# Earlier first loads in a diffusion-step kernel: w_ada and x weights of the heads in the shared stage, four expert blocks beside w_out, first picks between the first products

## The chip, the cores and the metric

The kernel runs on one core of a Trainium2 chip. Times are device microseconds of a whole execution of the program. The three runs of the kernel before took 2437.72, 2439.86 and 2441.40 us. The profile comes from a further execution, and its stage times are counted in microseconds from the start of its span.

## The reference

One layer of a network that mixes two kinds of state-space heads and ends in a mixture of experts is applied to a prompt of 128 tokens and to a sample of 256 tokens. All is float32, the model width D is 2048, and the prompt and the sample have modulation vectors of their own. In outline, for one token set x:

```
mod  = silu(cond) @ w_ada + b_ada                      # six vectors of 2048: shift, scale, gate, twice
h    = rms_norm(x) * (1 + scale_m) + shift_m
proj = h @ w_in                                        # widths: z 1024, x 1024, B and C 512, dt 32, then RWKV
y    = [ ssd_heads(z, conv(x), conv(B, C), dt),  rwkv7_heads(...) ]     # 16 + 16 heads, forward and backward
x    = x + gate_m * (y @ w_out)
h    = rms_norm(x) * (1 + scale_f) + shift_f
aff  = softmax(h @ router_w)                           # 16 experts
gate, idx = top_k(aff.T, 2 * n_tok / 16)               # each expert picks 16 prompt and 32 sample tokens
hid  = silu(h[idx] @ w_gate[e]) * (h[idx] @ w_up[e])   # 2048 -> 1024, for e = 0 .. 15
x    = x + gate_f * scatter_add((hid @ w_down[e]) * gate)
out  = rms_norm(x) * g                                 # besides: the final states of all heads
```

The weights of the experts are 16 x 24 blocks of 1024 KB (8 of gate, 8 of up and 8 of down for each expert), each read once.

## The kernel before, in words

The 384 tokens (T) are handled at once; activations lie with the channels on the 128 partitions. A large tile, `arena`, holds three tensors of 16 x 384 columns: `xT` (the residual), `mixed` (the outputs of all heads) and `hT` (the normed input). Each stage is a block with one instruction list for each engine, written out by hand: SP issues loads from its queue in the order of the code, POOL issues the w_ada loads of the heads from a software queue, and semaphores carry the waits. Between stages all engines meet at a barrier. A load that was issued before a barrier may land behind it, where its user waits for its semaphore.

The stages in order:

- **setup** (to about 106 us): reads the vectors, transposes x, and computes the first two modulation vectors from 32 blocks of w_ada.
- **ssd_shared** (106 to 222 us): projects dt, B, C and the low-rank inputs of RWKV. TensorE's `project(n, ...)` (L413 to L417) multiplies `w_shared` block n by `hT`; six blocks go through a ring of five (L377, L399 to L402), each with its semaphore `loaded[n]`. Then SP loads the first x and z weights of the heads into the two slots of `w_xz` (L403, L404). TensorE projects these at L449 to L453 (semaphores `x_proj`, `z_proj`). POOL only clears two tiles (L408, L409). `mixed` isn't in use before the heads write it.
- **ssd_heads** (222 to 515 us): eight turns, one for each pair of heads. In a turn TensorE does the x and z projections of the next pair (`feed`, 32 steps of K), the attention-like products of the pair, and, spread between them, eight `strips` of the remaining four modulation vectors: strip n multiplies `cond` by `wa[:, n % 4]`, one of four slots of w_ada blocks. POOL opens with twelve semaphore increments (`ahead`, the last one is `adah_col`, for which the first strip waits), then issues the loads: four at once, and each later one when a slot was used. SP opens with small loads (decay rows to memory and back: `seg`, `eac`), then loads the x weights of the second pair (`if c == 0`), then the second z weights, and so on in turn.
- **rwkv** (to about 1292 us): the second kind of heads; the first part of the w_out product is done in its last turns.
- **project_out** (1292 to 1430 us): the rest of the w_out product, 16 chunks of output channels through a ring of four (L1576), with residual, transposition back to tokens, and the router's products. SP issues the last load when chunk 11 is done, and then waits only for `gfin`.
- **experts** (1431 us to the end): `route()` ranks the tokens; `pick(g)` gathers the tokens of four experts by one-hot products, 16 steps of k, each evicted by VectorE (prompt part) and ScalarE (sample part) into `picked`; then for each expert `up` (8 steps kk, each with a gate and an up block), `turn`, `down` (8 blocks). The blocks run through a ring of 12 slots: 6 in `arena` (over `xT` and `mixed`) and 6 in `w_exp`. SP issues the load of block g when block g - 12 was used (`exp_used`, L1731 to L1737). `up(0)` waits for all 16 evictions of `pick(0)`:

```
                if e == 0 or e in PICK_AT:
                    pe.wait_ge(S("picked_c"), KC * (PICK_AT.get(e, 0) + 1))
                    pe.wait_ge(S("picked_s"), KC * (PICK_AT.get(e, 0) + 1))
```

Of the kernel before, what the change touches and what calls it, by code (L numbers as in the profile page):

```python
# [21 lines left out]
P = 128  # L22
D = 2048
KC = D // P
# [92 lines left out]
def program(nc, I, O, table, stop="all"):  # L117
# [17 lines left out]
    with ctx:  # L135
        ps = [ctx.enter_context(nc.psum_tensor(f"bank{n}", [P, 512], F32)) for n in range(8)]
        cst = sb(ctx, "cst", [P, CONST["row"][0]])
        par = sb(ctx, "par", [P, 352])
        modT = sb(ctx, "modT", [P, 96, 2])
        gain = sb(ctx, "gain", [P, 2, KC, 2])  # L140
        cond = sb(ctx, "cond", [P, KC, 32])
        arena = sb(ctx, "arena", [P, 3 * KC * T])
        xT, mixed, hT = (arena[:, n * KC * T:(n + 1) * KC * T].rearrange("p (k t) -> p k t", k=KC) for n in range(3))
        xtok = arena[:, 2 * KC * T:].rearrange("p (t d) -> p t d", t=TILES)

        def C(name, p0=0, p1=P):
            a, b = CONST[name]
            return cst[p0:p1, a:b]

        env = dict(nc=nc, I=I, O=O, table=table, S=S, sb=sb, ps=ps, cst=cst, par=par, modT=modT, gain=gain, xT=xT, C=C)  # L150
        with ExitStack() as proj:
            lora = sb(proj, "lora", [P, 3, T])
            w_narrow = sb(proj, "w_narrow", [P, KC, P])
            setup(**env, cond=cond, hT=hT, w_narrow=w_narrow)
            if stop == "ada":
                return
            ssd(**env, cond=cond, hT=hT, mixed=mixed, lora=lora, w_narrow=w_narrow)
            if stop == "ssd":
                return
            reuse_semaphores()  # L160
            rwkv(**env, hT=hT, mixed=mixed, lora=lora)
        reuse_semaphores()
        if stop == "rwkv":
            return
        with ExitStack() as ffn:
            acc = sb(ffn, "x_sum", [P, KC * T])
            late = dict(gates=sb(ffn, "gates", [P, D // 2]), gfin=sb(ffn, "gfin", [P, D]), shifts=sb(ffn, "shifts", [P, 48]),
                        acc=acc, sums=acc[:, 0:T], logits=acc[0:48, T:2 * T], xtok=xtok)
# [180 lines left out]


def ssd(nc, I, O, table, S, sb, ps, cst, par, modT, gain, xT, C, cond, hT, mixed, lora, w_narrow):

    w_in = I["w_in"].rearrange("l (k p) n -> p (l k) n", p=P)
    with ExitStack() as st:
# [11 lines left out]
        w_xz = sb(st, "w_xz", [P, 2, KC, P])  # L366
        ssd_shared(nc, I, S, sb, ps, par, modT, gain, xT, C, hT, lora, w_narrow, w_xz, w_in, B, Cm, Btok, BC, cum, ea, r7, tokq, cin, acc, sig)
        ssd_heads(nc, I, O, S, sb, ps, par, modT, C, cond, hT, mixed, w_xz, w_in, Cm, Btok, BC, cum, ea, r7, tokq, cin, acc, sig)


def ssd_shared(nc, I, S, sb, ps, par, modT, gain, xT, C, hT, lora, w_narrow, w_xz, w_in, B, Cm, Btok, BC, cum, ea, r7, tokq, cin, acc, sig):

# [3 lines left out]
    with ExitStack() as st:  # L376
        RING = 5  # L377
        w = sb(st, "w_shared", [P, RING, KC, P])
        dt = sb(st, "dt", [HEADS, 2, T])
# [14 lines left out]
        def _(sp):  # L394
# [16 lines left out]
        @block.tensor  # L411
# [163 lines left out]

def ssd_heads(nc, I, O, S, sb, ps, par, modT, C, cond, hT, mixed, w, w_in, Cm, Btok, BC, cum, ea, r7, tokq, cin, acc, sig):

    HG = KC // 4
    with ExitStack() as st:
# [14 lines left out]
        y = sb(st, "y", [P, T])  # L594
        AR, SLOTS_A = 4, 8
# [3 lines left out]
        w_ada = I["w_ada"].rearrange("l (k p) n -> p (l k) n", p=P)  # L599
        block = st.enter_context(nc.Block())  # L600
# [3 lines left out]
        def _(pool):  # L604
            ahead(pool, S, "z_proj", "hT_in", "sT_out", "s1_ready", "y_done", "xtok_in", "x_conv", "fin_out", "y_in", "adah_col")

            def load(c, n):
                src = w_ada[:, 2 * n:2 * n + 2, bass.ds(c * 1024 + 2 * D, 1024)]
                nc.gpsimd.dma_start(wa[:, n % AR], src).then_inc(ada_loaded[n % AR], 16)
# [19 lines left out]
        def _(sp):  # L629
# [917 lines left out]

def project_out(nc, I, O, table, S, sb, ps, cst, par, modT, gain, xT, C, mixed, gates, gfin, acc, sums, logits, shifts, xtok):

# [6 lines left out]
    with ExitStack() as st:  # L1556
# [15 lines left out]
        def _(sp):  # L1572
            for n in range(KC):
# [106 lines left out]

def experts(nc, I, O, table, S, sb, ps, cst, par, modT, gain, xT, C, arena, gates, gfin, acc, sums, logits, shifts, xtok):

# [9 lines left out]
    PICK_AT = {PACK * g: g for g in range(1, PACKS)}  # L1692
    wide = [I[n].rearrange("l e (q c p) n -> p (l e q) c n", p=P, c=2) for n in ("exp_w_gate", "exp_w_up")]
    tall = I["exp_w_down"].rearrange("l e (q p) n -> p (l e q) n", p=P)
    with ExitStack() as st:
        more = sb(st, "w_exp", [P, RING - HOME, 2048])
        w = [arena[:, n * 2048:(n + 1) * 2048] for n in range(HOME)] + [more[:, n] for n in range(RING - HOME)]
        picked = sb(st, "picked", [P, KC, PACK * SLOTS + PAD])
# [28 lines left out]
        def _(sp):  # L1727
            for e in range(N_EXP):
                for n in range(NS):
                    g = e * NS + n  # L1730
                    if g >= RING:  # L1731
                        sp.wait_ge(S("exp_used"), g - RING + 1)
                    if n < UPS:
                        dst, src = w[g % RING].rearrange("p (c n) -> p c n", c=2), wide[n % 2][:, e * 8 + n // 2]
                    else:
                        dst, src = w[g % RING], tall[:, e * 8 + n - UPS]
                    sp.dma_start(dst, src).then_inc(loaded[g % RING], 16)  # L1737
            for i in range(TILES * 4):
# [7 lines left out]
        def _(pe):  # L1746
            def arrived(e, n):
                g = e * NS + n
                pe.wait_ge(loaded[g % RING], (g // RING + 1) * 16)
                return w[g % RING]  # L1750
# [16 lines left out]

            def pick(g):

                pe.wait_ge(S("onehot"), min(g, 1) + 1)  # L1770
                if g:
                    pe.wait_ge(S("gu_out"), 2 * PACK * g)
                    pe.wait_ge(S("G"), PACK * g)
                for k in range(KC):
# [4 lines left out]
                    pe.matmul(ps[k % 2][:, 0:PACK * CAPC], xtok0(k), ohc[:, PACK * g:PACK * (g + 1)].rearrange("p e c -> p (e c)"), start=True, stop=True).then_inc(S("pick_c"), 1)  # L1779
                    for t in range(2):  # L1780
# [67 lines left out]
            route()  # L1848
            pick(0)
            for e in range(N_EXP):  # L1850
# [78 lines left out]
        def _(dve):  # L1929
# [43 lines left out]
            def pick(g):  # L1973
                for k in range(KC):
                    dve.wait_ge(S("pick_c"), KC * g + k + 1)
                    V.tensor_scalar(picked[:, k, 0:PACK * SLOTS].rearrange("p (e s) -> p e s", s=SLOTS)[:, :, 0:CAPC],
                                    ps[k % 2][:, 0:PACK * CAPC].rearrange("p (e c) -> p e c", e=PACK), gain[:, 1, k, 1:2], modT[:, 3 * KC + k, 1:2],
                                    ALU.mult, ALU.add).then_inc(S("picked_c"), 1)
# [93 lines left out]
```

## Time and profile before

| | |
|---|---|
| median of 3 runs | 2439.86 us (2437.72 to 2441.40) |
| profiled execution | 2442.29 us, its span 2440.6 us |
| TensorE busy (matmul) | 2173.0 us, 89% of the span |
| VectorE, ScalarE, POOL busy | 850.8, 393.6, 154.2 us |
| bytes read from memory | 586.89 MB |
| mean granted clock of TensorE | 0.963 of full speed |

The profile gives each engine's busy time, a chain of waits that ended last, and the start, duration and releaser of every instruction. [...]

### The profile page before, as it was taken

What the parts mean: (1) busy time and instruction counts of PE and PEld (TensorE: products, weight loads), DVE (VectorE), ACT (ScalarE), POOL (GpSimd) and SP (SyncE); (2) the same over time, 40 slices, a digit from 0 to 9 for tenths busy, and PEclk for the clock granted to TensorE, in tenths of its full rate; (3) what the DMA queues carried; (4) which work ended last, traced back from release to release, by engine and by line L of the source; (5) the groups of instructions that cost most, each with busy time, mean ns of one, the idle gap of its engine ahead of it and who ended that gap; (6) DMA issues with size and microseconds to landing.
All of it is one profiled execution on the core that took longest, in us unless ns stands there. A gap on an engine that the chain in (4) does not pass through costs nothing. (4 is left out here: it accounts for less than half of the span.)

```text
span 2440.6 us, 37768 instructions
## 1 busy us (share of the span) xinstructions
PE 2173.0 (89%) x16156; PEld 1108.7 (45%) x16156; DVE 850.8 (35%) x1816; ACT 393.6 (16%) x788; POOL 154.2 (6%) x185
## 2 busy tenths in 40 slices
PE   6786899979999999999997979889988898889886
PEld 2243455545666666666664543224322432243222
DVE  2262244334565566556542031212212221122113
ACT  1112121222222332322211120001000100010002
POOL 0000111110110010011010100000000000000000
PEclk9798999989999999999998989999999999999998
DMA  9933899943111111111103359999999999999996
GB/s 361 346 79 108 284 343 342 338 150 89 46 41 40 49 39 32 49 46 41 37 19 98 95 207 401 413 413 413 413 413 413 413 413 413 413 413 413 413 413 271
DMA packets 271135, 594.00 MB, mean 243 GB/s; under 512 B 25869, under 2 KB 166247, under 8 KB 249863
## 3 DMA queue, kind: packets, MB, share of 16 engines
q1 hardware_dynamic: 253575, 524.64, 57.6%
q0 software_dynamic: 17408, 67.11, 7.3%
q8 instruction: 122, 2.00, 0.3%
q14 instruction: 30, 0.25, 0.0%
HBM read 586.89 MB, written 4.82 MB: 242 GB/s over the span
## 5 line engine op out<-in xcount | busy, mean ns | idle before, releaser
L1816 PE MATMUL bank<-arena,picked 128*64 128x512 f32 x1280 | 303.2, 618 | 51.6 <-DMA arena<-exp_w_up 48.9
L1076 PE MATMUL bank<-arena,w_rkv 128*128 128x384 f32 x768 | 282.9, 505 | 8.1 <-DMA w_rkv<-w_in 8.1
L1995 DVE TENSOR_TENSOR x_sum<-x_sum,bank 128x512 f32<-128x512 f32 x180 | 115.4, 683 | 325.8 <-PE bank L1801 325.8
L1816 PEld LDWEIGHTS bank<-arena,picked 128*64 128x64 f32 x1280 | 98.2, 141 | 247.9 <-issue 247.1
L1840 PE MATMUL bank<-w_exp,hid 128*64 128x512 f32 x768 | 176.4, 597 | 6.7 <-DMA w_exp<-exp_w_down 6.7
L1816 PE MATMUL bank<-w_exp,picked 128*64 128x512 f32 x768 | 174.9, 597 | 7.4 <-DMA w_exp<-exp_w_up 6.8
L1076 PEld LDWEIGHTS bank<-arena,w_rkv 128*128 128x128 f32 x768 | 136.8, 191 | 95.7 <-issue 13.7
L690 PE MATMUL bank<-arena,w_xz 128*128 128x384 f32 x448 | 157.2, 499 | 15.3 <-DMA w_xz<-w_in 15.3
L1882 ACT COPY gu<-bank 112x512 f32<-112x512 f32 x32 | 17.2, 589 | 691.8 <-PE bank L1816 691.8
L690 PEld LDWEIGHTS bank<-arena,w_xz 128*128 128x128 f32 x448 | 82.4, 192 | 95.2 <-issue 30.2
L1608 PE MATMUL bank<-arena,w_out_ring 128*128 128x384 f32 x320 | 109.0, 497 | 12.5 <-DMA w_out_ring<-w_out 12.5
L1049 POOL TENSOR_TENSOR WI<-WX,cst 128x384 f32<-128x384 f32 x80 | 78.6, 998 | 645.5 <-DVE WX L1477 452.9
L1816 PEld LDWEIGHTS bank<-w_exp,picked 128*64 128x64 f32 x768 | 56.1, 136 | 122.0 <-issue 122.0
L1801 PE MATMUL bank<-outs,G 48*128 48x512 f32 x384 | 107.0, 638 | 1.4 <-DVE outs L2014 1.4
L1840 PEld LDWEIGHTS bank<-w_exp,hid 128*64 128x64 f32 x768 | 56.8, 136 | 111.8 <-issue 84.3
L2014 DVE TENSOR_TENSOR outs<-bank,gates 128x512 f32<-128x512 f32 x32 | 20.6, 686 | 236.8 <-PE bank L1840 236.8
L1608 PEld LDWEIGHTS bank<-arena,w_out_ring 128*128 128x128 f32 x320 | 60.9, 195 | 53.0 <-DMA w_out_ring<-w_out 13.2
L1500 DVE TENSOR_TENSOR WI<-WI,bank 128x384 f32<-128x384 f32 x80 | 44.1, 551 | 116.5 <-PE bank L1195 75.8
L705 PE MATMUL bank<-w_ada,cond 128*32 128x512 f32 x512 | 66.0, 621 | 20.1 <-DMA w_ada<-w_ada 17.3
L1069 PE MATMUL bank<-arena,w_rkv 128*128 128x384 f32 x192 | 74.2, 516 | 4.3 <-DVE arena L1456 4.3
L416 PE MATMUL bank<-arena,w_shared 128*128 128x384 f32 x192 | 64.6, 499 | 9.7 <-ACT cin L486 9.7
L1182 PEld LDWEIGHTS bank<-WI 64*64 64x64 f32 x1920 | 59.8, 135 | 27.2 <-issue 27.2
(370 smaller groups left out, 2632.9 us busy)
## 6 DMA issues: line engine op xcount, KB each, us to landing
w_exp<-exp_w_down SPq DMA_DIRECT2D x96, 1024.0 KB, 20.9
arena<-exp_w_gate SPq DMA_DIRECT2D x80, 1024.0 KB, 18.9
arena<-exp_w_up SPq DMA_DIRECT2D x80, 1024.0 KB, 19.1
w_ada<-w_ada POOLq DMA_DIRECT2D x64, 1024.0 KB, 8.2
w_exp<-exp_w_gate SPq DMA_DIRECT2D x48, 1024.0 KB, 18.3
w_exp<-exp_w_up SPq DMA_DIRECT2D x48, 1024.0 KB, 18.6
w_ada<-w_ada SPq DMA_DIRECT2D x32, 1024.0 KB, 17.8
arena<-exp_w_down SPq DMA_DIRECT2D x32, 1024.0 KB, 18.3
```

The costliest lines, as they stand in the source:

```text
L416: mm = pe.matmul(bank[:, 0:T], w[:, n % RING, k], hT[:, k], start=(k == 0), stop=(k == KC - 1))
L690: mm = pe.matmul(ps[j][:, 0:T], w[:, j, k], hT[:, k], start=(k == 0), stop=(k == KC - 1))
L705: mm = pe.matmul(ps[4][32 * j:32 * j + 32, :], cond[:, 2 * n + j // 2], wa[:, n % AR, j // 2, j % 2 * 512:(j % 2 + 1) * 512], start=(n == ...
L1049: nc.gpsimd.tensor_tensor(CT[d], W2[d][:, :, 2], m, ALU.mult).then_inc(S(f"CT_ready{d}"), 1)
L1069: mm = pe.matmul(ps[6][:, 0:T], w[:, m % 3, n % 8], mixed[:, n % 8], start=(n % 8 == 0), stop=(n % 8 == 7))
L1076: mm = pe.matmul(ps[feed_bank(i)][:, 0:T], w[:, m % 3, n % 8], hT[:, n % KC], start=(n % KC == 0), stop=(n % KC == KC - 1))
L1182: mm = pe.matmul(ps[3 * d][HP[1 - h], c * Q:(c + 1) * Q], CT[d][HP[h], c], X[d][HP[h], c], start=True, stop=True)
L1608: mm = pe.matmul(ps[n % BANKS][:, 0:T], w[:, n % RING, k], mixed[:, k], start=(k == first(n)), stop=(k == KC - 1))
L1801: pe.matmul(ps[bank + h][:], G[rows, t * P:(t + 1) * P], outs[rows, b], start=True, stop=True).then_inc(S("add_in"), 1)
L1816: mm = pe.matmul(ps[b][COLS[j], :], picked[:, k, at:at + 64], halves[j][:, c * 1024 + b * 512:c * 1024 + (b + 1) * 512], start=(k == 0), s ...
L1840: mm = pe.matmul(ps[4 + b][COLS[j], :], hid[:, f], wd[:, n * 512:(n + 1) * 512], start=(f == 0), stop=(f == 7))
L1995: V.tensor_tensor(y, y if e else x, ps[(LAST_BANKS[i // 2 % 4] if e == LAST else 6) + i % 2][:], ALU.add).then_inc(S("added"), 1)
```

## The change

Three things are moved, and one ring is made smaller.

1. In `ssd_shared` the ring of `w_shared` has three blocks instead of five and lies in `mixed`; SP waits for `bc_proj` before blocks 3, 4 and 5. The tile `wa` is allocated for the shared stage and the heads together. POOL loads the first four w_ada blocks of the heads in the shared stage, once the last `w_shared` block has landed. SP loads the x weights of the second pair in the shared stage, once the first x projection is done.
2. In `project_out` SP loads the first four expert blocks into a new tile, `w_early`, behind the w_out loads, and waits for them at the stage's end. In `experts` these are slots 0 to 3 of the ring, which stays at 12 slots: 4 in `w_early`, 6 in `arena`, 2 in `w_exp`.
3. `pick(0)` is cut: two steps of k before `up(0)`, and two before each of its steps kk but the last; step kk waits for the evictions of its own two k alone. The prompt part of `pick(0)` goes to banks 4 and 5, since `up(0)` accumulates in banks 0 and 1.

```diff
@@ program
             acc = sb(ffn, "x_sum", [P, KC * T])
+            w_early = sb(ffn, "w_early", [P, EARLY, 2048])
@@
+AR = 4
+def ada_rows(I, c, n):
+    return I["w_ada"].rearrange("l (k p) n -> p (l k) n", p=P)[:, 2 * n:2 * n + 2, bass.ds(c * 1024 + 2 * D, 1024)]
@@ ssd
+        wa = sb(st, "w_ada1", [P, AR, 2, 1024])
@@ ssd_shared
-        RING = 5
-        w = sb(st, "w_shared", [P, RING, KC, P])
+        RING = 3
+        w = mixed.rearrange("p k t -> p (k t)").rearrange("p (r k c) -> p r k c", r=RING, k=KC)
...
             for n, (c0, width) in enumerate(COLS):
-                if n == RING:
+                if n >= RING:
                     sp.wait_ge(S("bc_proj"), n - RING + 1)
                 sp.dma_start(w[:, n % RING, :, 0:width], w_in[:, :, c0:c0 + width]).then_inc(loaded[n], 16)
             for j, name in enumerate("xz"):
                 sp.dma_start(w_xz[:, j], w_in[:, :, 1024 * (1 - j):1024 * (1 - j) + P]).then_inc(S(f"w{name}_loaded"), 16)
+            sp.wait_ge(S("x_proj"), 1)
+            sp.dma_start(w_xz[:, 0], w_in[:, :, 1024 + P:1024 + 2 * P]).then_inc(S("wx_loaded"), 16)
...
             nc.gpsimd.memset(lp[:], 0.0).then_inc(S("pads_zero"), 1)
+            pool.wait_ge(loaded[len(COLS) - 1], 16)
+            for n in range(AR):
+                nc.gpsimd.dma_start(wa[:, n], ada_rows(I, 0, n)).then_inc(S(f"adah_loaded{n}"), 16)
@@ ssd_heads
-        wa = sb(st, "w_ada1", [P, AR, 2, 1024])
...
-            for n in range(SLOTS_A):
-                if n >= AR:
-                    pool.wait_ge(S("adah_used"), n - AR + 1)
+            for n in range(AR, SLOTS_A):
+                pool.wait_ge(S("adah_used"), n - AR + 1)
                 load(0, n)
...
-                if c == 0:
-                    sp.wait_ge(S("x_proj"), 1)
-                    load_w(0, 1)
@@ project_out
+            block = expert_rows(I)
+            for n in range(EARLY):
+                sp.dma_start(w_early[:, n].rearrange("p (c n) -> p c n", c=2), block(0, n)).then_inc(S("early_loaded"), 16)
             sp.wait_ge(S("gfin_loaded"), 16)
+            sp.wait_ge(S("early_loaded"), 16 * EARLY)
@@ experts
-        more = sb(st, "w_exp", [P, RING - HOME, 2048])
-        w = [arena[:, n * 2048:(n + 1) * 2048] for n in range(HOME)] + [more[:, n] for n in range(RING - HOME)]
+        more = sb(st, "w_exp", [P, RING - HOME - EARLY, 2048])
+        w = [w_early[:, n] for n in range(EARLY)] + [arena[:, n * 2048:(n + 1) * 2048] for n in range(HOME)] + [more[:, n] for n in range(RING - HOME - EARLY)]
...
+                    if g < EARLY:
+                        continue
                     if g >= RING:
                         sp.wait_ge(S("exp_used"), g - RING + 1)
...
-                pe.wait_ge(loaded[g % RING], (g // RING + 1) * 16)
+                if g >= EARLY:
+                    pe.wait_ge(loaded[g % RING], (g // RING + (g % RING >= EARLY)) * 16)
...
-            def pick(g):
+            def pick(g, k0=0, k1=KC):
+                bank = 0 if g else 4
...
-                if e == 0 or e in PICK_AT:
-                    pe.wait_ge(S("picked_c"), KC * (PICK_AT.get(e, 0) + 1))
-                    pe.wait_ge(S("picked_s"), KC * (PICK_AT.get(e, 0) + 1))
+                if e in PICK_AT:
+                    pe.wait_ge(S("picked_c"), KC * (PICK_AT[e] + 1))
+                    pe.wait_ge(S("picked_s"), KC * (PICK_AT[e] + 1))
                 at = e % PACK * SLOTS
                 for kk in range(8):
+                    if e == 0:
+                        if kk < 7:
+                            pick(0, 2 * kk + 2, 2 * kk + 4)
+                        pe.wait_ge(S("picked_c"), 2 * kk + 2)
+                        pe.wait_ge(S("picked_s"), 2 * kk + 2)
                     halves = [arrived(e, 2 * kk + j) for j in range(2)]
...
             route()
-            pick(0)
+            pick(0, 0, 2)
```

`EARLY` is 4; `expert_rows(I)` returns a function that gives the memory region of block n of expert e, as the loop over the loads did before.

## Rows read from the trace of the kernel before

**Rows 1.** The page's 40 equal slices of the span (61 us each): transfer rate.
```profile
GB/s 361 346 79 108 284 343 342 338 150 89 46 41 40 49 39 32 49 46 41 37 19 98 95 207 401 413 413 413 413 413 413 413 413 413 413 413 413 413 413 271
```
**Rows 2.** Chain that ended last, experts: start us, us, what.
```profile
1460.93 27.71 PE bank L1816 x128
...
2390.35 24.91 DMA w_exp<-exp_w_down
```
**Rows 3.** Timeline, heads: start, us, engine, line, operation, tiles, count [idle before, releaser].
```profile
223.94 3.02 POOL L609 DMA_DIRECT2D w_ada<-w_ada  x4 [115.23 <-issue]
...
230.77 1.94 PE L705 MATMUL bank<-w_ada,cond 128*32 128x512 f32 x8 [9.40 <-DMA w_ada<-w_ada]
231.02 15.77 SPq L632 DMA_DIRECT2D w_xz<-w_in  x2
...
234.44 1.94 PE L705 MATMUL bank<-w_ada,cond 128*32 128x512 f32 x8 [1.73 <-DMA w_ada<-w_ada]
...
251.71 9.85 PE L690 MATMUL bank<-arena,w_xz 128*128 128x384 f32 x24 [15.34 <-DMA w_xz<-w_in]
...
286.00 1.92 PE L705 MATMUL bank<-w_ada,cond 128*32 128x512 f32 x16 [0.35 <-DVE modT L835]
...
297.64 4.14 PE L690 MATMUL bank<-arena,w_xz 128*128 128x384 f32 x12
...
320.30 1.92 PE L705 MATMUL bank<-w_ada,cond 128*32 128x512 f32 x16 [0.35 <-DVE modT L835]
```
**Rows 4.** Stretches: length, busy us (instructions) of five engines, granted clock, DMA share, GB/s.
```profile
160.00:180.00 20.00, 17.32 (x48) 10.08 (x49) 12.79 (x26) 3.87 (x10) 0.00 (x0) 0.83 0.00 0
...
226.00:252.00 26.00, 4.16 (x17) 0.70 (x18) 5.21 (x16) 6.02 (x9) 2.38 (x4) 0.50 1.04 344
...
237.00:245.00 8.00, 0.00 (x0) 0.00 (x0) 3.24 (x12) 2.09 (x4) 0.42 (x1) 0.50 1.05 356
...
350.00:382.00 32.00, 31.64 (x156) 16.31 (x154) 14.77 (x37) 7.39 (x13) 4.99 (x7) 1.00 1.00 339
```
**Rows 5.** Timeline, shared stage, TensorE.
```profile
132.11 20.91 PE L416 MATMUL bank<-arena,w_shared 128*128 128x384 f32 x64
...
162.68 9.66 PE L416 MATMUL bank<-arena,w_shared 128*128 128x384 f32 x23 [9.66 <-ACT cin L486]
...
199.24 20.91 PE L452 MATMUL bank<-arena,w_xz 128*128 128x384 f32 x64 [0.57 <-ACT BC L495]
```
**Rows 6.** DMA issues: tiles, engine, operation, count, size, median us to landing.
```profile
w_shared<-w_in SPq DMA_DIRECT2D x6, 1024.0 KB, 10.5
```
**Rows 7.** DMA, 222 to 290 us: slices of 1.7 us; queues: packets, MB, share.
```profile
GB/s 22 49 200 354 390 285 343 414 415 400 330 342 331 383 360 296 290 290 303 349 28 0 0 0 24 248 410 414 354 291 351 397 406 350 221 417 417 174 88 112
...
q0 software_dynamic: 3278, 12.64, 51.5%
...
q1 hardware_dynamic: 9197, 5.74, 31.3%
```
**Rows 8.** Timeline, w_out stage and the start of the experts.
```profile
1314.42 66.32 SPq L1576 DMA_DIRECT2D w_out_ring<-w_out  x11
...
1416.16 10.49 PE L1608 MATMUL bank<-arena,w_out_ring 128*128 128x384 f32 x32
...
1430.82 0.37 SPq L1737 DMA_DIRECT2D arena<-exp_w_gate  x1
```
**Rows 9.** Timeline, first picks and the first load behind a freed slot.
```profile
1446.31 0.69 PE L1779 MATMUL bank<-ohc,arena 128*128 128x64 f32 x2 [1.64 <-DVE ohs L1970]
...
1451.03 0.41 PE L1779 MATMUL bank<-ohc,arena 128*128 128x64 f32 x2
...
1464.58 0.37 SPq L1737 DMA_DIRECT2D arena<-exp_w_gate  x1
```
**Rows 10.** Stretches, where the expert stream pauses.
```profile
1463.00:1464.00 1.00, 1.00 (x8) 0.38 (x6) 0.66 (x4) 0.00 (x0) 0.00 (x0) 1.00 0.32 115
...
1466.00:1467.00 1.00, 1.00 (x7) 0.38 (x5) 0.00 (x0) 0.00 (x0) 0.00 (x0) 1.00 0.62 238
```

More of the change, by code:

```diff
@@ L366, in ssd, with ssd_shared @@
         w_xz = sb(st, "w_xz", [P, 2, KC, P])
[L367 to L371 removed]
+        wa = sb(st, "w_ada1", [P, AR, 2, 1024])
+        ssd_shared(nc, I, S, sb, ps, par, modT, gain, xT, C, hT, lora, w_narrow, mixed, w_xz, wa, w_in, B, Cm, Btok, BC, cum, ea, r7, tokq, cin, acc, sig)
+        ssd_heads(nc, I, O, S, sb, ps, par, modT, C, cond, hT, mixed, w_xz, wa, w_in, Cm, Btok, BC, cum, ea, r7, tokq, cin, acc, sig)
+def ssd_shared(nc, I, S, sb, ps, par, modT, gain, xT, C, hT, lora, w_narrow, mixed, w_xz, wa, w_in, B, Cm, Btok, BC, cum, ea, r7, tokq, cin, acc, sig):
     COLS = [(2048 + n * P, P) for n in range(4)] + [(N_SSD_IN + 3072, P), (N_SSD_IN + 3264, P)]
     with ExitStack() as st:
[L377 to L378 removed]
+        RING = 3
+        w = mixed.rearrange("p k t -> p (k t)").rearrange("p (r k c) -> p r k c", r=RING, k=KC)
         dt = sb(st, "dt", [HEADS, 2, T])
@@ L573, in _, with ssd_heads @@
             link(nc.vector.tensor_scalar(dst[:, 1], dst[:, 1], -1.0, None, ALU.mult))
-def ssd_heads(nc, I, O, S, sb, ps, par, modT, C, cond, hT, mixed, w, w_in, Cm, Btok, BC, cum, ea, r7, tokq, cin, acc, sig):
+def ssd_heads(nc, I, O, S, sb, ps, par, modT, C, cond, hT, mixed, w, wa, w_in, Cm, Btok, BC, cum, ea, r7, tokq, cin, acc, sig):
     HG = KC // 4
@@ L594, in ssd_heads @@
         y = sb(st, "y", [P, T])
-        AR, SLOTS_A = 4, 8
-        wa = sb(st, "w_ada1", [P, AR, 2, 1024])
+        SLOTS_A = 8
         arow = sb(st, "arow1", [P, 512])
         ada_loaded = [S(f"adah_loaded{n}") for n in range(AR)]
-        w_ada = I["w_ada"].rearrange("l (k p) n -> p (l k) n", p=P)
         block = st.enter_context(nc.Block())
@@ L607, in load @@
             def load(c, n):
[L608 to L613 removed]
+                nc.gpsimd.dma_start(wa[:, n % AR], ada_rows(I, c, n)).then_inc(ada_loaded[n % AR], 16)
+            for n in range(AR, SLOTS_A):
+                pool.wait_ge(S("adah_used"), n - AR + 1)
                 load(0, n)
@@ L1545, in _, with expert_rows, block, project_out @@
             end(PAIRS - 1)
-def project_out(nc, I, O, table, S, sb, ps, cst, par, modT, gain, xT, C, mixed, gates, gfin, acc, sums, logits, shifts, xtok):
+EARLY = 4
+def expert_rows(I):
+    wide = [I[n].rearrange("l e (q c p) n -> p (l e q) c n", p=P, c=2) for n in ("exp_w_gate", "exp_w_up")]
+    tall = I["exp_w_down"].rearrange("l e (q p) n -> p (l e q) n", p=P)
+    def block(e, n):
+        return wide[n % 2][:, e * 8 + n // 2] if n < 16 else tall[:, e * 8 + n - 16]
+    return block
+def project_out(nc, I, O, table, S, sb, ps, cst, par, modT, gain, xT, C, mixed, gates, gfin, w_early, acc, sums, logits, shifts, xtok):
     RING, BANKS = 4, 3
@@ L1678, with experts @@
 PACK = 4
-def experts(nc, I, O, table, S, sb, ps, cst, par, modT, gain, xT, C, arena, gates, gfin, acc, sums, logits, shifts, xtok):
+def experts(nc, I, O, table, S, sb, ps, cst, par, modT, gain, xT, C, arena, gates, gfin, w_early, acc, sums, logits, shifts, xtok):
     HOME = 2 * KC * T // 2048
@@ L1692, in experts @@
     PICK_AT = {PACK * g: g for g in range(1, PACKS)}
-    wide = [I[n].rearrange("l e (q c p) n -> p (l e q) c n", p=P, c=2) for n in ("exp_w_gate", "exp_w_up")]
-    tall = I["exp_w_down"].rearrange("l e (q p) n -> p (l e q) n", p=P)
+    rows = expert_rows(I)
     with ExitStack() as st:
-        more = sb(st, "w_exp", [P, RING - HOME, 2048])
-        w = [arena[:, n * 2048:(n + 1) * 2048] for n in range(HOME)] + [more[:, n] for n in range(RING - HOME)]
+        more = sb(st, "w_exp", [P, RING - HOME - EARLY, 2048])
+        w = [w_early[:, n] for n in range(EARLY)] + [arena[:, n * 2048:(n + 1) * 2048] for n in range(HOME)] + [more[:, n] for n in range(RING - HOME - EARLY)]
         picked = sb(st, "picked", [P, KC, PACK * SLOTS + PAD])
@@ L1730, in _ @@
                     g = e * NS + n
+                    if g < EARLY:
+                        continue
                     if g >= RING:
                         sp.wait_ge(S("exp_used"), g - RING + 1)
[L1733 to L1737, printed above, removed]
+                    dst = w[g % RING].rearrange("p (c n) -> p c n", c=2) if n < UPS else w[g % RING]
+                    sp.dma_start(dst, rows(e, n)).then_inc(loaded[g % RING], 16)
             for i in range(TILES * 4):
@@ L1766, in route @@
                 mm.then_inc(S("rank_T"), 1)
-            def pick(g):
[L1770 to L1774, printed above, removed]
+            def pick(g, k0=0, k1=KC):
+                bank = 0 if g else 4
+                if k0 == 0:
+                    pe.wait_ge(S("onehot"), min(g, 1) + 1)
+                    if g:
+                        pe.wait_ge(S("gu_out"), 2 * PACK * g)
+                        pe.wait_ge(S("G"), PACK * g)
+                for k in range(k0, k1):
                     i = KC * g + k
@@ L1778, in pick @@
                         pe.wait_ge(S("picked_s"), i - 1)
-                    pe.matmul(ps[k % 2][:, 0:PACK * CAPC], xtok0(k), ohc[:, PACK * g:PACK * (g + 1)].rearrange("p e c -> p (e c)"), start=True, stop=True).then_inc(S("pick_c"), 1)
+                    pe.matmul(ps[bank + k % 2][:, 0:PACK * CAPC], xtok0(k), ohc[:, PACK * g:PACK * (g + 1)].rearrange("p e c -> p (e c)"), start=True, stop=True).then_inc(S("pick_c"), 1)
                     for t in range(2):
```

4 lines of the change are left out of this document (2 added, 2 removed).

## The prediction

> **What bounds the kernel now.** I read the view of 40 slices first [rows 1], then the chain of waits [rows 2], then timelines and tables of stretches at the three places that the change touches. Two stages move most of the bytes, and they are limited in different ways. In the experts (from 1431 us on) the transfers run at 413 GB/s in every slice but the first and the last [rows 1], and the chain ends with a DMA block that lands at 2415.3; only the last expert's tail of some 25 us follows [rows 2]. So there the end is set by when the stream starts, and by whether it runs dry. TensorE waits for blocks now and then; its own work is not the bound. In the heads (222 to 515 us) a turn takes 34.30 us, from the first w_ada strip of one turn (286.00) to that of the next (320.30) [rows 3], and TensorE hardly idles in it (31.64 of 32 us) [rows 4]; but the first turn takes 55 us, because it opens on empty buffers. These are the two places where time can be had: the slow first turn, and the dry stretch of the stream at the start of the experts.
>
> **The shared stage: a smaller ring, and what is loaded behind it.** The ring of w_shared goes from 5 blocks to 3 and moves into mixed, which nobody reads or writes before the heads. Blocks 3, 4 and 5 now wait for projections 0, 1 and 2. A projection takes 10.4 us (20.91 for two), so these end near 131, 142.6 and 153; projection 3 begins at 162.7, the next two some 12 and 22 us later [rows 5]. A block lands a median of 10.5 us after its issue [rows 6], 10 us or more ahead of use: cost 0. Queued on SP behind the new waits are the two w_xz blocks, now issued near 153; of the same size and kind, they are in by 174 at the worst and due at 199.2 [rows 5]: cost 0. Without that margin TensorE would stall for the excess, microsecond by microsecond. POOL then issues the first four w_ada blocks (3.02 us of issue) near 163, behind nothing but two memsets; DMA is idle there (0.00 from 160 to 180) [rows 4] and they are needed at 224: 60 us for 4.2 MB. Last, SP waits for x_proj and issues the second x weights near 209.7 (half of 20.91 after 199.24), 12 us before the stage ends; nothing is queued behind it but the barrier, which needs its issue and not its landing.
>
> **The heads' first turn.** Three stalls of TensorE go: 9.40 us before the first strip, 1.73 before the second, 15.34 before the x weights [rows 3]. Of the first one 2.5 us stay: the strip waits for the last of POOL's opening semaphore increments, and POOL's first load went out right behind these, at 223.94, where PE's last work was at 221.4 (230.77 less 9.40) [rows 3]. So 6.9 + 1.7 + 15.3 = 23.9 us go. Clock: from 226 to 252 the granted clock was 0.50, the lower level [rows 4]; two strips took 3.88 us there and 1.92 later, and 24 matmuls took 9.85 where twelve take 4.14 later [rows 3], 3.5 us in all. One such restart stays, 1.8. The new turn would end at 223.9 + 34.3 + 1.8 = 260.0 instead of 286.0: 26.0 earlier.
> What is late next? The second z weights. SP issues them where the x weights went out, at 231.0; TensorE wants them 14.4 us into a turn (297.64 plus two thirds of 4.14, less 286.00) and 1.8 for the clock: 240.1. From about 227 the queues hold two w_ada blocks (2.10 MB), seg (0.79), eac (0.26) and z (1.05); these 4.2 MB take 11.8 us at 356 GB/s [rows 4], so z lands at 238.8. I take no stall, with 6 us as the far end (rival A). Behind that the DMA has little room: a full turn moves 11.8 MB in 34.3 us, and its share is 1.00 at 339 GB/s [rows 4]; the first turn has its own seg and eac on top, 1.05 MB or 2.9 us. I charge 2 of these: 24.0 us. A second account, by bytes: 5.24 MB leave the stage, 15.5 us at 339 GB/s, and the stretch in which the queues ran dry, four slices of 1.7 us near nothing [rows 7], closes: 22.3. I take 23.5, as the stalls are the more direct row; bounds 14 (z as late as x was, 20.7 us after its issue) and 26. Later turns have the same work, and RWKV starts its own loads behind the barrier, so the gain is passed on whole.
>
> [...] The rows: from 222 to 290 the software queue moved 12.64 MB in 3278 packets, 3.9 KB each, SP's queue 5.74 MB in 9197, 0.6 KB each [rows 7], and the old x block was the last of its batch to arrive, at 251.7 [rows 3]. [...]
>
> **Four expert blocks beside w_out.** SP's last w_out block is issued near 1380.7 (66.32 us after 1314.42); the four loads go behind it, 10.2 us at 413 GB/s, and land near 1393. TensorE starts on the last w_out block at 1416, and the stage ends at 1430.8 [rows 8]. Cost 0; without that cover, 10.2. SP's four issues (0.37 us the first) leave the start of the experts.
>
> **Picks between the first products.** Before, 16 picks ran from 1446.31 to 1460.93, then the first products, and the first slots came free with SP's issue at 1464.58 [rows 2, 9]. Twelve blocks had arrived by about 1463.3: the stream fell to 115 GB/s there and was back at rate after 1466.4 [rows 10]. Now four picks go ahead; the fifth started at 1451.03 [rows 9], so the first products start there, 9.9 us sooner, and slots are free near 1454.7. The eight blocks still to load end near 1453, so the stream restarts at 1456.5. The 372 blocks after that are the same in both kernels, 2.54 us each: 9.9 us at the end if it never runs dry again. Pace: eight steps of products take 27.71 us [rows 2], 3.46 each; with two picks of 0.83 (the last twelve, 1451.03 to 1460.93) 5.11, and two blocks take 5.08. So it just holds. I charge 0.15 us at each of six seams: gain 9, with 4 and 12.5 as bounds (rival B and beyond; no dry stretch at all). Full slots don't stop the stream later: near 1489 some 24.5 blocks have come and 16 are used, and the 5.5 us to the next release bring 2.2 more, 10.7 ahead of 12. TensorE's work on this expert is only reordered; ScalarE's and VectorE's picks wait for nothing new, and banks 4 and 5 are free until the down products.
>
> **Sum.** 23.5 + 9 = 32.5 us. The profiled execution took 2442.29 us (span 2440.6): 2409.8. The runs' median, 2439.86, is 2.4 lower, so **2407 us**.
>
> **The rivals.**
> A. Z is late, behind w_ada blocks 6 and 7. It arrives when POOL's next 2.1 MB, issued near 239, are through, 6 us at 356 GB/s, near 246: stall 6, gain 26.5, 2413. For: the x block's arrival at the end [rows 3]. Against: those two loads go out only when z should have landed.
> B. The interleaved picks break the pace. At the mean of the first four (1446.31 to 1451.03, 1.18 each [rows 9]) a step takes 5.82 against 5.08, and six steps lose 4.4: gain 29, 2411; at twice the warm time, all 9 go and it is 2416. For: pairs of short picks between long products. Against: TensorE doesn't idle long there, so the clock should hold.
> C. The heads' part doesn't act: the later turns give the time back, as their DMA share is 1.00 [rows 4]. 9 us remain: 2431. Against: TensorE hardly waits in these turns.
> D. Slower. The expert stream gets a lower rate in the new order of slots (w_early in front, fewer in w_exp). Each of 372 blocks pays; at 2.63 us instead of 2.54 (399 GB/s) the 32.5 us are eaten, below 397 it is slower by over 0.2%, at 390 it is 2463. Against: 413 in all slices, whichever slots were in turn [rows 1].
>
> **How the numbers follow.** Forecast 0.62 (its own range 2402 to 2410.5), A 0.15, B 0.11, C 0.05, D 0.03; 0.04 for gains beyond 38 us. The range of 8 in 10 takes in A and B and the bounds of the unknown costs: 2399 to 2418. A measurement of this kernel can tell about 0.2%, 5 us, from no change. Faster: the forecast, A, B, C and the larger gains, less a little for what I overlooked: 0.95; same 0.02; slower 0.03.
>
> **What would show it.** In the trace after: the first w_ada strip near 224; the second turn's first strip near 262; no wait of more than 3 us for w_xz; a w_out stage as long as before; the first products some 20 us after the experts' first load instead of 30; the stream at rate again some 26 us after that load, with no second gap over 1 us. It is wrong if the turns of 34.3 us get longer, if the expert stream isn't at 413 GB/s, or if the early blocks lengthen the w_out stage.

## The result and the profile after

The changed kernel takes 2415.15 us (median of four runs, 2412.62 to 2417.60) against 2440.5 for the kernel before beside it (four runs): a ratio of 0.9898 (95% interval 0.9882 to 0.9914; intervals stand in brackets below), a gain of 25 us where 33 were forecast. The profiled execution took 2416.78 us, its span 2415.1, so 25.5 less than the span of before. These 25.5 us can be placed by four stretches that both kernels have, from the start of the span to its end. The shared stage's start is ScalarE's first instruction there (106.83 before, 104.59 after):

| stretch | before | after | gain |
|---|---|---|---|
| setup, code unchanged | 106.83 | 104.59 | 2.2 |
| shared stage's start to the second turn's first strip | 179.17 | 163.83 | 15.3 |
| from there to the experts' first load | 1144.82 | 1143.30 | 1.5 |
| experts' first load to the end | 1009.8 | 1003.4 | 6.4 |

The first line is scatter: in the ten profiles of this study, all with the same setup, the shared stage began between 104.59 and 106.83. So is the third: over the same profiles that stretch took 1140.2 to 1144.8 us, and with the heads as before it took 1142.6, 1142.7 and 1144.8 (experts_only, picks_only, early_only, see below). The change is the second line and the fourth.

The heads first. This is the timeline of the kernel after (start, us, engine, line, operation, tiles, count, idle before and its releaser), the stretch that answers to [rows 3] and [rows 5]:

```profile
157.79 3.02 POOL L424 DMA_DIRECT2D w_ada<-w_ada  x4 [51.31 <-DMA arena<-w_in]
...
208.07 0.37 SPq L416 DMA_DIRECT2D w_xz<-w_in  x1
...
221.56 2.62 PE L713 MATMUL bank<-w_ada,cond 128*32 128x512 f32 x16 [1.98 <-POOLq L102]
...
224.51 0.71 POOL L621 DMA_DIRECT2D w_ada<-w_ada  x1 [0.83 <-PE bank L713]
...
228.91 0.66 SPq L643 DMA_DIRECT2D w_xz<-w_in  x1
...
233.00 1.93 PE L713 MATMUL bank<-w_ada,cond 128*32 128x512 f32 x16
...
234.40 1.57 POOL L621 DMA_DIRECT2D w_ada<-w_ada  x2 [9.18 <-PE bank L713]
...
237.21 3.24 DVE L808 SCALAR_TENSOR_TENSOR M<-seg,tokq,cst 128x128 f32<-128x128 f32 x12 [8.71 <-DMA seg<-rows_cum]
...
246.80 2.93 PE L698 MATMUL bank<-arena,w_xz 128*128 128x384 f32 x4 [9.10 <-DMA w_xz<-w_in]
...
268.42 1.92 PE L713 MATMUL bank<-w_ada,cond 128*32 128x512 f32 x16 [0.35 <-DVE modT L843]
```

The numbers behind x count the trace's records. A step of these float32 products has two: before, L416 has x192 for the six blocks of 16 steps of `w_shared`, and L690 x448 for 7 x 32 steps of `feed`. So z, step 17 of a turn's 32, comes behind 32 records, the 24 and then 8 of the 12 of [rows 3], which is the prediction's two thirds of 4.14. A load's row stands under the engine that issued it and gives the time of the issue: 3.02 us for POOL's four at 157.79, 0.66 for z on SP.

The old first wait is down to 1.98 us, the x wait is gone, and a wait of 9.10 for the second z block stands in their place: issued at 228.91, it is there at 246.7, 17.8 us later. Between the two, at 234.40, POOL has issued w_ada blocks 6 and 7. The turn takes 46.86 us; a full one still takes 34.30, so 12.56 are lost. The windows (length, busy us of five engines, granted clock, DMA share, GB/s) give the rest of it, beside [rows 4]:

```profile
221.00:231.00 10.00, 9.44 (x35) 4.47 (x36) 3.66 (x7) 4.47 (x7) 1.43 (x2) 0.83 0.76 213
231.00:241.00 10.00, 6.71 (x31) 2.78 (x29) 3.24 (x12) 2.08 (x4) 1.43 (x2) 1.00 1.12 316
241.00:251.00 10.00, 4.20 (x15) 2.00 (x15) 0.63 (x2) 0.01 (x1) 0.00 (x0) 0.66 0.96 309
```

The granted clock is below full at the opening (0.83, and 0.50 from 223 to 226) and again after TensorE has waited (0.66, and 0.50 from 246.8 to 249.7). The first strips with their 24 records of feed take 11.44 us (221.56 to 233.00) where an undisturbed turn takes 9.79: 1.65. The four records behind the wait take 2.93 instead of 1.56, and with the products next to them 1.8 are lost there. 9.10 + 1.65 + 1.80 = 12.55. The 1.65 were lost before z was due, so they aren't z's.

Then the experts, the timeline that answers to [rows 8, 9]:

```profile
1361.68 1.27 SPq L1605 DMA_DIRECT2D w_early<-exp_w_gate  x1
...
1397.06 10.49 PE L1634 MATMUL bank<-arena,w_out_ring 128*128 128x384 f32 x32
...
1411.72 0.37 SPq L1761 DMA_DIRECT2D arena<-exp_w_gate  x1
...
1427.21 0.69 PE L1807 MATMUL bank<-ohc,arena 128*128 128x64 f32 x2 [1.65 <-DVE ohs L2003]
...
1431.87 3.65 PE L1849 MATMUL bank<-w_early,picked 128*64 128x512 f32 x16
...
1435.54 0.37 SPq L1761 DMA_DIRECT2D w_early<-exp_w_gate  x1
...
1436.98 3.65 PE L1849 MATMUL bank<-w_early,picked 128*64 128x512 f32 x16
...
1442.10 3.65 PE L1849 MATMUL bank<-arena,picked 128*64 128x512 f32 x16
```

The w_out stage is as long behind its last block as before (14.66 us from 1397.06 to the first expert load, 14.66 before). The first freed slot is refilled 23.82 us after that load, 33.76 before: 9.94 sooner. Steps of two products and two picks come every 5.11 to 5.12 us. The stage as a whole gains 6.4, and the chain still ends with a block of the last expert, beside [rows 2]:

```profile
2358.36 3.67 PE bank L1849 x16
2362.38 27.37 DMA w_exp<-exp_w_down
```

It lands at 2389.75, 978.0 us after the first load (984.4 before). Windows of the stream after the restart, beside [rows 10]:

```profile
1437.00:1470.00 33.00, 32.67 (x173) 14.57 (x172) 6.84 (x22) 5.29 (x12) 0.00 (x0) 1.00 1.00 397
1470.00:1500.00 30.00, 27.80 (x131) 9.38 (x131) 6.41 (x16) 3.13 (x6) 0.00 (x0) 1.00 1.02 410
```

Against 413 that is (16 x 33 + 3 x 30) / 413 = 1.5 us. The end of the stream holds the rest. This is the transfer rate in slices of 0.5 us around the last landing, before (2400 to 2420 us) and then after (2375 to 2395):

```profile
GB/s 377 459 410 410 459 377 442 426 426 442 377 442 410 426 459 377 344 328 229 295 262 197 262 213 180 197 164 197 164 16 0 0 0 0 0 0 0 0 0 0
```

```profile
GB/s 393 442 393 442 426 410 459 377 442 410 360 295 262 295 295 229 246 197 213 229 180 180 98 33 33 16 33 16 16 0 0 0 0 0 0 0 0 0 0 0
```

Before, the rate drops from 164 over 16 to nothing. After, it falls to 33 and 16 for another 3 us, and from 2387 to 2389.5 the mean is 23 GB/s at a DMA share of 0.06. By my estimate that is about one of the sixteen engines that the share counts (1 / 16 = 0.06, 413 / 16 = 26); the rows don't name an engine. So the stream's lead of 9.9 us ends as 6.4: about 1.5 in the pace behind the restart, about 2 in an end that trails.

### The profile page after: what moved, and what is told of

It reads as the page before. It is cut to its first block and busy times, and to the rows that moved or that the text cites. A ratio compares the mean times of both kernels' runs of the same rounds, so it can differ in the third digit from the quotient of the medians.

```text
span 2415.1 us, 37774 instructions
## 1 busy us (share of the span) xinstructions
PE 2164.7 (90%) x16156; PEld 1103.5 (46%) x16156; DVE 850.5 (35%) x1816; ACT 393.6 (16%) x788; POOL 154.2 (6%) x185
## 5 line engine op out<-in xcount | busy, mean ns | idle before, releaser
L1849 PE MATMUL bank<-w_early,picked 128*64 128x512 f32 x1024 | 240.4, 614 | 46.0 <-DMA w_early<-exp_w_up 43.9
L1873 PE MATMUL bank<-arena,hid 128*64 128x512 f32 x768 | 171.9, 596 | 13.1 <-issue 11.3
L1849 PE MATMUL bank<-arena,picked 128*64 128x512 f32 x768 | 175.4, 598 | 4.6 <-DMA arena<-exp_w_up 4.1
L1849 PEld LDWEIGHTS bank<-w_early,picked 128*64 128x64 f32 x1024 | 77.8, 140 | 200.5 <-issue 200.2
L1849 PEld LDWEIGHTS bank<-arena,picked 128*64 128x64 f32 x768 | 54.1, 136 | 119.2 <-issue 118.8
L1873 PEld LDWEIGHTS bank<-arena,hid 128*64 128x64 f32 x768 | 60.6, 137 | 102.3 <-issue 100.3
L431 PE MATMUL bank<-arena 128*128 128x384 f32 x192 | 64.3, 497 | 9.7 <-ACT cin L501 9.7
```

What stands on the lines that cost most here:

```text
L431: mm = pe.matmul(bank[:, 0:T], w[:, n % RING, k], hT[:, k], start=(k == 0), stop=(k == KC - 1))
L1849: mm = pe.matmul(ps[b][COLS[j], :], picked[:, k, at:at + 64], halves[j][:, c * 1024 + b * 512:c * 1024 + (b + 1) * 512], start=(k == 0), s ...
L1873: mm = pe.matmul(ps[4 + b][COLS[j], :], hid[:, f], wd[:, n * 512:(n + 1) * 512], start=(f == 0), stop=(f == 7))
```

## The experiments

**The two halves.** heads_only keeps the change in the shared stage and the heads and takes back the experts' part; experts_only is the reverse.

```
heads_only:   - EARLY = 4 ... sp.dma_start(w_early[:, n] ...)   + the experts stage of before
experts_only: - RING = 3 (in mixed), early w_ada and second x   + RING = 5, loads in the heads, as before
```

> The w_ada blocks and x weights loaded in the shared stage alone; w_early and the cut picks undone. In the changed kernel's profile the heads, from the start of the shared stage to the second turn, took 15.4 us less than before. If this term is what the profile shows, the whole time falls by 15 to 17 us (ratio 0.9932 +- 0.0010). If my forecast of 23.5 us was right and the profiled execution was unlucky: 22 to 25 us, ratio 0.990.

> The early expert blocks and the cut picks alone; the shared stage and the heads as before. Theory 1 (the stream restarts 9.9 us earlier and the end follows; the 3.5 us missing in the changed kernel's profile are that one execution's): 8.5 to 10 us less, ratio 0.9963. Theory 2 (about 1 us goes to the step of products with picks, and 2.5 us to the last blocks, which one straggling DMA engine delivers later the longer the stream runs without a pause): 6 to 7 us less, ratio 0.9973.

Beside a kernel before of 2441.31 us, heads_only took 2424.95 us, 0.9929 [0.9916, 0.9943], by the ratio 17 us less; experts_only took 2433.14, 0.9970 [0.9959, 0.9981], 7 us less. The halves add up to the whole (24.6 of 25), so within the intervals neither disturbs the other, and both are below their terms of 23.5 and 9. The waits of TensorE in heads_only from 219 to 300 us (us in total, times, longest) show the same place as in the whole change:

```profile
PE bank L697 <- DMA w_xz<-w_in: 9.6, 1, 9.6
PE bank L712 <- POOLq L102: 2.0, 1, 2.0
```

In experts_only the stream restarts 24.73 us after its first load, 9.0 sooner than before, and its last block lands at 2405.55, 977.9 us after the first load, as long as in the whole change (two rows of its timeline, one of its chain):

```profile
1427.63 0.37 SPq L1754 DMA_DIRECT2D arena<-exp_w_gate  x1
...
1452.36 0.37 SPq L1754 DMA_DIRECT2D w_early<-exp_w_gate  x1
...
2380.66 24.89 DMA w_exp<-exp_w_down
```

**Is the late z block the heads' whole loss?** z_shared issues the second z block behind the second x block, in the shared stage:

```
             sp.dma_start(w_xz[:, 0], w_in[:, :, 1024 + P:1024 + 2 * P]).then_inc(S("wx_loaded"), 16)
+            sp.wait_ge(S("z_proj"), 1)
+            sp.dma_start(w_xz[:, 1], w_in[:, :, P:2 * P]).then_inc(S("wz_loaded"), 16)
...
-                    load_w(1, c + 1)
+                    if c:
+                        load_w(1, c + 1)
```

> The changed kernel, with the second z weights loaded in the shared stage too, as soon as the first z projection is done (near 218 us). Theory 1 (z was late because it stood behind seg and eac in SP's queue and beside POOL's loads): z lands before 228, the wait of 9.1 us goes, and the second turn starts at 37 to 39 us after the first strip instead of 46.9; 8 to 9 us less than the changed kernel, about 33 less than before, ratio 0.9865. Rival (the DMA engines are full, so z's megabyte only pushes seg and the w_ada blocks back): the stall moves to the w_ada strips or to the one-hot decays M, and less than 4 us are gained.

It took 2407.03 us, 0.9862 [0.9847, 0.9877]: 34 us less than before and 8 less than the change by the medians; it beats both kernels. Its timeline:

```profile
220.76 0.37 SPq L418 DMA_DIRECT2D w_xz<-w_in  x1
...
223.93 1.92 PE L716 MATMUL bank<-w_ada,cond 128*32 128x512 f32 x16 [1.98 <-POOLq L102]
...
237.76 3.24 DVE L811 SCALAR_TENSOR_TENSOR M<-seg,tokq,cst 128x128 f32<-128x128 f32 x12 [6.89 <-DMA seg<-rows_cum]
...
258.23 1.92 PE L716 MATMUL bank<-w_ada,cond 128*32 128x512 f32 x16 [0.36 <-DVE modT L846]
```

The first turn takes 34.30 us (223.93 to 258.23), the length of a full one. Block z, issued at 220.76 before POOL had anything in its queue, was there in 6.0 us. So 10.9 of the 12.56 us hang on that block: the wait of 9.10 and the 1.80 behind it. The 1.65 at the opening don't: the first strip runs at 1.92 here behind the same 1.98 us of idle time, but it does so in heads_only too (222.35 to the second turn at 268.76, 46.41 us), where z is late.

**Why is z late: POOL's loads, slow seg transfers ahead of it, or bytes?** Three kernels move one thing each. pool_late holds POOL's four blocks until z has landed, pool_late67 only blocks 6 and 7, and z_first puts z ahead of seg in SP's queue:

```
pool_late:    +            pool.wait_ge(S("wz_loaded"), 32)        # ahead of the loop over n
pool_late67:  +                if n == 6:
              +                    pool.wait_ge(S("wz_loaded"), 32)
z_first:      +            sp.wait_ge(S("z_proj"), 2)              # ahead of the seg loads
              +            load_w(1, 1)
              -                    load_w(1, c + 1)                 # at its old place
              +                    if c:
              +                        load_w(1, c + 1)
```

> The changed kernel, with POOL's loads of w_ada blocks 4 to 7 of the first turn held back until the second z weights have landed, so that SP's queue is alone meanwhile. Not a better kernel: strips 4 to 7 then wait. What counts is when seg and z land. Theory A (POOL's 4 KB rows take turns with SP's short ones, and crowd them out): seg within 6 us of its last issue, z within 5 us of its issue (17.8 us in the changed kernel), about 234. Theory B (seg, which reads one row of memory 128 times, is slow by itself and z stands behind it): seg's end and z move by less than 4 us, z near 243. Theory C (bytes alone, 356 GB/s): 2.1 MB of SP's own, z near 233.

> The changed kernel, with only POOL's w_ada blocks 6 and 7 of the first turn held until the second z weights have landed. Theory A (POOL's long rows crowd out SP's short ones while they are in flight): seg still lands near 13 us after its first issue, beside blocks 4 and 5, but z lands some 11 us after its issue instead of 17.8, near 240; the wait of 9.1 us falls to 2 to 4 and blocks 6 and 7 are still in time: 5 to 6 us less than the changed kernel, ratio to before 0.9875. Rival (what delays z are the loads in front of it in its own queue): z as late as before, blocks 6 and 7 later still, so slower than the changed kernel by some 3 us.

> The changed kernel, with the second z weights issued in the heads ahead of seg and eac instead of behind them, near 223.5. Theory A: z shares the engines with w_ada blocks 4 and 5 and lands within 12 us, near 235, before its use at 238; seg is pushed to 240 and the one-hot decays with it, so that the turn's xq product waits 2 to 4 us; second turn 37 to 40 us after the first strip (46.9 in the changed kernel, 34.3 in a full turn). If z landed after 240 in front of the queue too, the order in the queue has nothing to do with it.

The five kernels by the rows of their profiles (us; the stretch goes from the shared stage's start to the second turn's first strip, as in the first table, 179.2 before; the turn is its part from the first strip on, as the shared stage ahead of that varies from 115.5 to 117.9):

| kernel | z issued | landed after | VectorE's wait for seg | TensorE's wait for z | stretch | first turn |
|---|---|---|---|---|---|---|
| after | 228.91 | 17.8 | 8.71 | 9.10 | 163.8 | 46.86 |
| pool_late | 230.26 | 6.4 | 2.40 | none | 160.2 | 43.79 |
| pool_late67 | 228.42 | 13.1 | 8.28 | 4.05 | 158.0 | 42.54 |
| z_first | 225.54 | 12.5 | 10.06 | none | 156.0 | 38.45 |
| z_shared | 220.76 | 6.0 | 6.89 | none | 152.2 | 34.30 |

Without POOL's blocks, in pool_late, z lands in 6.4 us though it goes out later (theory A had said 5), and the four seg transfers take 3.0 to 5.7 us where they took 6.0 to 11.7. SP's transfers, then, are not slow by themselves, and theory B falls. Nor do SP's own bytes need 17.8 us. These are the rates at which pool_late moved them from 225.0 to 236.7 us, up to z's landing, in slices of 0.29 us (by theory C z was to come near 233):

```profile
GB/s 126 63 103 61 179 147 152 210 179 231 387 299 273 236 326 294 213 60 53 201 152 83 84 168 205 207 296 294 341 343 334 319 303 285 303 119 65 19 0 0
```

In the kernel after, the queues from z's issue to its landing (229.0 to 246.6 us: packets, MB, share of 16 engines' time) show what stood beside it:

```profile
q1 hardware_dynamic: 3795, 2.80, 61.7%
q0 software_dynamic: 816, 3.15, 46.4%
```

POOL's queue moved 3.15 MB in rows of 3.9 KB on the mean, SP's 2.80 MB in rows of 0.7 KB, 5.95 MB in all. Of SP's, some 0.9 MB belong to the next seg and x loads, issued behind z from 240.48 on: by 240 its queue had moved 2.26 MB since 222, about as much as z and all that stood ahead of it (1.05 for z, 0.79 for seg, 0.26 for eac, 0.13 for the h loads). Yet z landed only at 246.7. Two short windows show what held it, and seg before it. The first is 225 to 227 us, just behind the issue of POOL's blocks 4 and 5; the second is 240 to 243, where blocks 6 and 7 pass:

```profile
q0 software_dynamic: 164, 0.67, 91.3%
q1 hardware_dynamic: 1, 0.00, 0.0%
```

```profile
q0 software_dynamic: 308, 1.20, 101.1%
q1 hardware_dynamic: 17, 0.01, 1.0%
```

In both, POOL's blocks take nearly all of the engines' time (a share sums the packets' own times, so it can pass 100%), and SP's queue all but stands still. Holding POOL back has its own price, as the timeline of pool_late shows:

```profile
232.48 3.24 DVE L809 SCALAR_TENSOR_TENSOR M<-seg,tokq,cst 128x128 f32<-128x128 f32 x12 [2.40 <-DMA seg<-rows_cum]
...
236.95 2.84 POOL L621 DMA_DIRECT2D w_ada<-w_ada  x4 [75.01 <-DMA w_xz<-w_in]
...
245.71 1.93 PE L714 MATMUL bank<-w_ada,cond 128*32 128x512 f32 x8 [6.47 <-DMA w_ada<-w_ada]
```

Now the strip waits for its block, 6.47 us. Its one run took 2414.19 us. pool_late67 halves the wait for z (4.05 us, z landing in 13.1 where 11 were expected), so blocks 6 and 7 are part of it and not all:

```profile
241.59 1.67 PE L700 MATMUL bank<-arena,w_xz 128*128 128x384 f32 x4 [4.05 <-DMA w_xz<-w_in]
...
242.11 1.42 POOL L621 DMA_DIRECT2D w_ada<-w_ada  x2 [16.99 <-DMA w_xz<-w_in]
```

Its turn is 4.3 us shorter than that of after, but its median of 2413.20 (0.9890 [0.9875, 0.9906]) can't be told from the change's, where 5 to 6 us less were expected. z_first has no z wait and pays with seg, which now stands behind z (one run, 2407.99 us, which is too few for a verdict):

```profile
240.72 3.25 DVE L811 SCALAR_TENSOR_TENSOR M<-seg,tokq,cst 128x128 f32<-128x128 f32 x12 [10.06 <-DMA seg<-rows_cum]
...
245.89 2.07 PE L736 MATMUL bank<-Btok,xq 128*128 128x128 f32 x8 [2.14 <-DVE xq L818]
```

So the block is late because of POOL's blocks: it takes 6.4 us without any of them, 13.1 beside blocks 4 and 5, and 17.8 beside all four. What is put later in the two queues is late instead. Of the kernels tried, only z_shared, with an issue ahead of all that, pays nothing. No run changed the length of a row or the kind of a queue, so it isn't shown that POOL's blocks crowd out the others because their rows are longer.

**What in the experts gives the 7 us?** early_only loads the four blocks beside w_out and leaves all 16 picks ahead of the first product; picks_only interleaves the picks and loads nothing early. Both have the shared stage and the heads of before, as experts_only has.

```
early_only:   picks: for k in range(KC) ahead of up(0), as before;  EARLY loads kept
picks_only:   -            for n in range(EARLY):
              -                sp.dma_start(w_early[:, n] ...
```

> The four early expert blocks without the cut picks: pick 0 is whole, as before; shared stage and heads as before. Theory (the end follows from when the stream restarts, and that hangs on the first freed slot): the stream only runs dry 10 us earlier and restarts at the same 35.5 us after the stage's first load; no gain, within 0.2% of before. Rival (four blocks fewer in the stage are four blocks less at the end): 10 us less, ratio 0.9958.

> The cut picks without early blocks: twelve slots in arena and w_exp as before, the first products 9.9 us earlier. Theory: twelve blocks keep the stream busy until 32.5 us after the first load, and slots come free at 24, so it doesn't run dry at all: the 3 us gap goes and nothing else, 2.5 to 3.5 us less, ratio 0.9988. Rival (the 7 us that both parts gained are the picks' alone): ratio 0.997.

Beside a kernel before of 2441.01 us, early_only took 2442.21 us, 0.9999 [0.9990, 1.0008]; picks_only took 2436.84, 0.9988 [0.9979, 0.9997]. Apart they give 0 and 3 us, together 7. The rates of early_only and then of picks_only from 1425 to 1485 us, in slices of 1.5 us, show why:

```profile
GB/s 0 0 0 0 76 358 421 434 407 421 410 410 410 404 418 407 401 418 202 8 0 0 0 0 11 5 0 221 415 423 421 418 404 418 431 421 437 410 426 421
```

```profile
GB/s 0 0 96 410 410 429 421 407 410 415 407 410 410 410 410 407 407 421 404 410 412 407 410 407 407 421 399 412 404 429 399 437 437 431 415 399 415 437 437 426
```

In early_only the eight blocks that are left are through near 1453, and the stream stands still for 12 us, until the first slot comes free, 33.8 us after the first load as before:

```profile
1464.51 0.37 SPq L1754 DMA_DIRECT2D w_early<-exp_w_gate  x1
```

The four blocks loaded early are lost again in the pause. In picks_only the slot is free at 1452.25, 24.8 us after the first load:

```profile
1452.25 0.37 SPq L1748 DMA_DIRECT2D w_early<-exp_w_gate  x1
```

Twelve blocks last for 30 us, so the pause of before (some 3 us) is gone, and the rest of the earlier slot has nothing to act on. The stream restarts at the later of two events, the last block's arrival and the first free slot, and each edit moves one of them.

## Why the prediction was right or wrong

The direction, the places and the experts' mechanism were right; the gain was taken 8 us too large. The median stands inside the range given (2399 to 2418) and above the forecast's own (2402 to 2410.5). Two of the prediction's own signs failed: the second turn's first strip came at 268.42 where 262 was said, and there was a wait of 9.10 us for w_xz where none was to be over 3.

- **Setup behind the waits of SP and POOL, ring of 3, the early loads (cost 0).** Right. TensorE shows no stall for w_shared, POOL's four loads went out at 157.79, x at 208.07, and the w_out stage kept its 14.66 us behind the last block.
- **The three stalls that go (23.9) and the opening wait that stays (2.5).** Right: 1.98 stayed, and the first strip came 116.97 us into the stage where it was 123.94.
- **"z lands at 238.8. I take no stall".** This is the step that failed. It divided all bytes in flight by one rate from z's point of view, as if z came when 4.2 MB were through, 7.8 us after its issue, with POOL's blocks 6 and 7 issued after that. But beside blocks 4 and 5 alone z took 13.1 us (pool_late67); in after it was still in flight when blocks 6 and 7 were issued at 234.40, its last part stood still while they passed, and it took 17.8. Rival A was the case, and dearer than its 6 us: the wait was 9.10, and rival A had left out the 1.8 us that the lower clock cost behind it. That z came at 246.7 where rival A said 246 is in part luck: this execution's heads began 2.2 us earlier than the prediction counts, so rival A's 246 is 243.8 here, and z, due at 237.7, was 2.9 later than that. The old x block's late arrival, rival A's own ground, pointed the right way: z took 17.8 us beside POOL's queue and 6.4 (pool_late) and 6.0 (z_shared) without it. How the engines' time was dealt between the two queues isn't shown, only that SP's queue had 1.0% of the engines' time from 240 to 243 and POOL's 101.1%.
- **"I charge 2" for the backlog.** Not seen: the turns behind the first keep 34.30 us in after, and z_shared's first turn has 34.30 too. The restart at the lower clock (1.8) was there in after (1.65) and pool_late67, whose first strips took 2.62 and 2.69 and whose clock went to 0.50 there (223 to 226 and 223 to 225), and not in heads_only, pool_late, z_first and z_shared (1.92, the clock 1.00 from 221 to 227); the rows don't say why, as the idle time before the strip is 1.98 in all six.
- By these corrections the heads' sum is 26.0 - 9.1 - 1.8 = 15.1; measured 15.3. With z in time it is 27.0, z_shared's stretch. That this kernel's 2407.03 is the time that was forecast for the change is in part luck: the heads gave more than the 23.5 charged for them, and the experts less than their 9.
- **The stream's restart, 9.9 us.** Right: 9.94. The pace of 5.11 against 5.08 was right too.
- **"0.15 us at each of six seams", gain 9.** Too small a charge: 6.4 came out (experts_only 978 us from first load to last landing too, its gain by time 7). In after some 1.5 us went in the pace and 2 in the end that trails. In experts_only the restart came 9.0 us sooner and not 9.9, the rate behind it was lower (394 and 402 GB/s where after has 397 and 410, in windows that begin as long after the restart: 2.3 us), and its end didn't trail. So the length of 978 us repeats and its split doesn't; what causes the loss wasn't settled. That one straggling engine delivers the later the longer the stream runs (theory 2 of experts_only) isn't shown: experts_only's stream ran 953 us from its restart to its last landing and had no tail, that of after 954 us and had one.
- Rivals B, C and D fell: the steps with picks took 5.11 us and not 5.82; from the second turn to the experts nothing was given back (1143.30 us where it was 1144.82, within the scatter); and the stream ran at 413 GB/s in the slices of both kernels.

The page's rates answer to [rows 1]:

```profile
GB/s 365 342 157 109 309 336 341 324 118 73 49 39 32 51 47 42 40 42 38 37 20 107 157 219 406 412 413 413 413 413 413 413 413 413 413 413 413 413 413 254
```

## What to carry to other kernels

When a stall on one transfer is removed, work out the next transfer's arrival from what each queue will have in flight until it is complete, not from the bytes ahead of it at its issue; a load that flies beside another queue's large blocks should be issued before those (z took 6.0 us ahead of POOL's blocks and 17.8 beside them). Where a stream waits for both data and a free slot, move both: either edit alone may be worth nothing, as 0 and 3 us became 7 here. And look at what is issued at the end of a stage with idle queues: one more block moved there (z_shared) was worth 8 us.

## What the runs showed of the hardware

The 1 MB z block took 6.0 us (z_shared) and 6.4 (pool_late) without POOL's blocks in flight and 17.8 beside them (after; rows of 0.7 KB on the mean in SP's queue, 3.9 KB in POOL's), and the four transfers of 192 KB ahead of it took 6.0 to 11.7 us in after and 3.0 to 5.7 in pool_late. From 240 to 243 us POOL's blocks had 101.1% of the engines' time and SP's queue 1.0%. In the 17.6 us of z's flight SP's queue took 61.7% of the engines' time for 2.80 MB and POOL's 46.4% for 3.15 MB, so a byte of SP's queue cost 1.5 times the engine time of one of POOL's. When the granted clock was 0.50 the two first strips took 3.88 us (before) and at 1.00 1.92. And a stream at 413 GB/s over 970 us ended with 3 us at 33 and 16 GB/s in after and with 2 in z_shared, while the kernel before and experts_only ended without such a tail.
